# Three branch and output weight blocks loaded into the attention's room ahead of the row gathers, and heads 4 to 7 of both token halves projected from one load

## What is computed

```python
q, k, v, z, gl = split_proj(h @ w_in[l])
y = mix_branches(...)         # attention, gating; then @ w_branch_attn, w_branch_sgu, w_out
x_new = x + gt1 * rmsnorm(y, g_post_mix[l])
h2 = modulate(rmsnorm(x_new, g_pre_ffn[l]), sh2, sc2)
x = x_new + gt2 * rmsnorm(peer(h2, ...), g_post_ffn[l])

# peer: 8 heads, 256 queries wide each, 16 experts a head for every token
q = rmsnorm((xt @ w_query).reshape(T, 8, 2, 128))
s = einsum('thpd,pnd->thpn', q, sub_keys)
s1, i1 = top_k(s[:, :, 0], 16);  s2, i2 = top_k(s[:, :, 1], 16)
best, pos = top_k(all 256 sums s1 + s2, 16)
gate = softmax(best)
act = gelu(einsum('td,thkd->thk', x, u_tab[idx])) * gate
out = einsum('thk,thkd->td', act, v_tab[idx])
```

## Time and profile before

| | us |
|---|---|
| median of three runs | 2205.68 |
| lowest, highest | 2204.83, 2207.36 |
| the profiled execution, its whole time | 2205.23 |
| its span in the trace | 2203.4 |
| first row issued, last data of the rows | 1486, 2184 |

### The profile page before, as it was taken

How to read it: one execution, slowest core, us unless ns; L and a number is a source line. 1 busy time by engine, 2 the same in 40 slices (tenths; PEclk the granted TensorE clock), 3 DMA queues, 4 the chain that set the end, 5 groups by cost and what they waited for, 6 DMA issues and landing times.

```text
span 2203.4 us, 24558 instructions
## 1 busy us (share of the span) xinstructions
PE 1490.9 (68%) x10272; PEld 620.2 (28%) x10272; DVE 753.4 (34%) x1892; ACT 434.0 (20%) x992; POOL 291.8 (13%) x265
## 2 busy tenths in 40 slices
PE   8888766767775665666659999997756744344344
PEld 7554311322221111111114454555323511001000
DVE  5823101000000000000013143345657676876774
ACT  1321110000000000000011174342333232323221
POOL 0000000000000000000000000003434445444341
PEclk9988877888898878777879999998867865655555
DMA  9549999999999999999994346449999999999996
GB/s 387 210 174 397 427 426 426 426 428 427 427 427 427 427 427 426 427 427 427 427 418 162 152 185 235 178 166 410 422 421 402 419 420 420 417 420 419 419 419 279
DMA packets 75870, 814.24 MB, mean 370 GB/s; under 512 B 8464, under 2 KB 8592, under 8 KB 9840
## 3 DMA queue, kind: packets, MB, share of 16 engines
q1 hardware_dynamic: 38704, 544.03, 59.3%
q0 software_dynamic: 36864, 268.45, 29.4%
q10 hardware_dynamic: 192, 0.20, 0.0%
HBM read 811.40 MB, written 1.05 MB: 369 GB/s over the span
## 4 chain that ended last, share of the span: by engine, by line
DMA 48%; PE 33%; DVE 12%; ACT 4%; issue 2%; POOL 2%; ACTq 0%; DVEq 0%; POOLq 0%
DMA AR<-in_w_down 18%; DMA AR<-in_w_up 15%; DMA AR<-in_peer_uv,AR 14%; PE PS L396 13%; DVE AR L1384 3%; PE PS L624 3%; PE PS L829 3%; PE PS L645 2%; PE PS L787 2%; PE PS L407 2%; POOL AR L1761 2%; PE PS L511 1%; DVE AR L906 1%; DVE AR L908 1%; PE PS L657 1%
## 5 line engine op out<-in xcount | busy, mean ns | idle before, releaser
L1761 POOL DMA_INDIRECT AR<-in_peer_uv,AR x256 | 290.0, 1133 | 1704.9 <-DVE AR L1375 1438.3
L829 PE MATMUL PS<-AR 32*32 32x512 f32 x4096 | 233.2, 944 | 328.8 <-ACT AR L1720 328.8
L624 PE MATMUL PS<-AR 128*32 128x512 f32 x2048 | 301.9, 726 | 187.1 <-DMA AR<-in_w_up 131.9
L1384 DVE CUSTOM_DVE_ANT_0 AR<-AR 128x1024 f32<-128x1024 f32 x256 | 309.5, 1222 | 154.1 <-DMA AR<-in_peer_uv,AR 154.1
L396 PE MATMUL PS<-AR 128*128 128x512 f32 x736 | 330.8, 605 | 1.9 <-DVE AR L881 1.9
L645 PE MATMUL PS<-AR 128*32 128x512 f32 x1024 | 174.7, 818 | 102.4 <-DMA AR<-in_w_down 94.9
L1080 DVE TENSOR_TENSOR AR<-AR,PS 128x512 f32<-128x512 f32 x16 | 11.0, 688 | 596.6 <-PE PS L624 596.6
L396 PEld LDWEIGHTS PS<-AR 128*128 128x128 f32 x736 | 140.1, 195 | 173.2 <-issue 172.6
L624 PEld LDWEIGHTS PS<-AR 128*32 128x32 f32 x2048 | 63.2, 121 | 414.2 <-DMA AR<-in_w_up 207.5
L829 PEld LDWEIGHTS PS<-AR 32*32 32x32 f32 x4096 | 43.9, 128 | 474.1 <-ACT AR L1720 461.7
L1094 DVE COPY AR<-PS 128x512 f32<-128x512 f32 x16 | 11.1, 692 | 282.9 <-PE PS L645 282.9
(11 more groups left out here) (273 smaller groups left out, 1251.1 us busy)
## 6 DMA issues: line engine op xcount, KB each, us to landing
AR<-in_w_gate SPq DMA_DIRECT2D x64, 2048.0 KB, 26.1
AR<-in_w_up SPq DMA_DIRECT2D x64, 2048.0 KB, 25.7
AR<-in_w_down SPq DMA_DIRECT2D x64, 2048.0 KB, 26.4
AR<-in_w_in SPq DMA_DIRECT2D x29, 2048.0 KB, 7.8
AR<-in_w_ada SPq DMA_DIRECT2D x12, 2048.0 KB, 9.8
AR<-in_peer_w_query SPq DMA_DIRECT2D x8, 2048.0 KB, 11.9
AR<-in_w_out SPq DMA_DIRECT2D x6, 2048.0 KB, 11.5
AR<-in_w_branch_sgu SPq DMA_DIRECT2D x4, 2048.0 KB, 7.7
```

The costliest lines, as they stand in the source:

```text
L624: x = pe.matmul(PS[32 * q:32 * q + 32, bk, :], XS[:, j, e * 32:(e + 1) * 32], IN[key][:, jj, q * 512:(q + 1) * 512], start=(j == 0), stop= ...
L829: x = pe.matmul(PS[c:c + 32, ACC[a][g], :], DI[t, p, r, :], AR[t, off + 1024 + m * 512:off + 1536 + m * 512], start=(h == 0 and p == 0), s ...
L1384: v.tensor_tensor_reduce(rows, rows, HB[:, a, :], 1.0, 0.0, MULT, ADD, DOT[:, ix, k:k + 1]).then_inc(*w.hit("dot", ix, k))
L1761: pool.indirect_dma_start(out=AR[:, off:off + 2048], out_offset=None, in_=D["peer_uv_2"], in_offset=bass.IndirectOffsetOnAxis(ap=EI[:, ix, ...
```

## The change

What it does:

- Three loads, `w_branch_attn` 0 and 1 and `w_out` 0 for half 1, are issued as soon as the last attention head is done, ahead of the first row, into the places at W0, o and o + 16384. These hold the four row buffers of before.
- The row buffers in the beginning are instead one at o + 21120 and the eight halves of four weight slots: two slots that held query blocks 0 and 1, and two that held `w_branch_sgu` for half 1. That is nine again; a tenth comes after `yt` of half 1, and three more at `rt0` of item 8.
- Query blocks 2 and 3 (heads 4 to 7) are loaded once and used for both halves; the last load serving them is freed only by half 1. Blocks 0 and 1 are still loaded twice.
- `late` begins with the tail; the queries follow, first heads 4 to 7 with the halves alternating, then heads 0 to 3 of half 1, each `qs` joined with the next `qm`. 25 entries, popped after rows 0 to 72; the twelve queries stand after rows 30 to 63. `back` and `gain2` of half 1 are last.
- From the first row on there are five weight loads: `w_out` 1, query blocks 2 and 3, query blocks 0 and 1 again.

```diff
-        place = [NARENA + i * SLOT for i in range(NS)] + [W0, SPARE, o + 21120, o + 14336]
+        place = [NARENA + i * SLOT for i in range(NS)] + [W0, SPARE, o + 21120, o + 14336, o, o + 16384]
...
-            late = queries(2, 0) + queries(3, 0) + [h[0], h[1] + h[2]]
+            late = [h[0], h[1] + h[2]]
             late += [b[0][0], b[0][1] + b[1][0], b[1][1] + y[0], p[0][0], p[0][1] + p[1][0], p[1][1] + u[0], u[1] + u[2], u[3] + u[4]]
-            late += queries(0, 1) + [[("gain2",)], [("back", 1)]] + queries(1, 1) + queries(2, 1) + queries(3, 1)
+            late += queries(*[(h, a) for h in range(4, 8) for a in range(2)], *[(h, 1) for h in range(4)]) + [[("back", 1)], [("gain2",)]]
...
-            free = {k: ("mm", "av", 15) for k in (o + 2048, W0 + 2048, o + 16384, o + 18432)}
-            free[o + 21120] = ("gsb", 1, 1)
-            free.update({k: ("used", "wq", i, 0) for i in range(2) for k in halves[i]})
+            free = {o + 21120: ("gsb", 1, 1)}
+            for i, event in ((0, ("wq", 0, 0)), (2, ("w_bs", 0, 1)), (3, ("w_bs", 1, 1)), (1, ("wq", 1, 0))):
+                free.update({k: ("used", *event) for k in halves[i]})
...
-                key = ("wq", n, a)
+                key = ("wq", n, a if n < 2 else 0)
...
+                    for n in range(2):
+                        square(("wq", n, 0), "peer_w_query_2", n)
+                    w.wait_ge("mm", "av", 15)
+                    for slot, key, name, n in ((NS, "w_ba", "w_branch_attn_2", 0), (NS + 4, "w_ba", "w_branch_attn_2", 1),
+                                               (NS + 5, "w_op", "w_out_2", 0)):
+                        load(slot, (key, n, 1), weight(name, n), 8, 512)
+                    turn[0], ids[0] = 0, [NS, NS + 5]
-                elif stage == "ba":
+                elif stage == "ba" and x[1] == 0:
...
-                elif stage == "op":
+                elif stage == "op" and x != [0, 1]:
...
-                elif stage == "qm" and x[0] % 2 == 0:
+                elif stage == "qm" and (x in ([4, 0], [6, 0]) or x[0] in (0, 2) and x[1] == 1):
```

More of the change, by code:

```diff
@@ L289, in mixer_order, with queries @@
             steps(*u[2:4], pairs[9], u[4], pairs[10])
[L291 to L305, removed]
+            def queries(*heads):
+                parts = [[("qm", *heads[0])]]
+                for x, y in zip(heads, heads[1:]):
+                    parts.append([("qs", *x), ("qm", *y)])
+                return parts + [[("qs", *heads[-1])]]
             h, b, y, p, u = tail(1)
-            late = queries(2, 0) + queries(3, 0) + [h[0], h[1] + h[2]]
+            late = [h[0], h[1] + h[2]]
             late += [b[0][0], b[0][1] + b[1][0], b[1][1] + y[0], p[0][0], p[0][1] + p[1][0], p[1][1] + u[0], u[1] + u[2], u[3] + u[4]]
-            late += queries(0, 1) + [[("gain2",)], [("back", 1)]] + queries(1, 1) + queries(2, 1) + queries(3, 1)
+            late += queries(*[(h, a) for h in range(4, 8) for a in range(2)], *[(h, 1) for h in range(4)]) + [[("back", 1)], [("gain2",)]]
             todo += [("take", 0), ("qm", 0, 0), ("qs", 0, 0), ("rt0", 0)]
-            q = queries(0, 0)
-            for x in q[2:] + [[("back", 0)]]:
-                todo += x
+            todo += [("qm", 1, 0), ("qs", 1, 0), ("back", 0)]
             todo += [(f"rt{s}", 0) for s in range(1, 6)]
@@ L318, in mixer_order @@
             assert not then
-            for x in queries(1, 0):
-                todo += x
+            todo += [("qm", 2, 0), ("qs", 2, 0), ("qm", 3, 0), ("qs", 3, 0)]
             routes = []
@@ L343, in build @@
         ORDER = mixer_order()
+        HEADS = [tuple(x) for stage, *x in ORDER if stage == "qm"]
         RING = [5, 2, 3, 4]
@@ L352, in row_places @@
             halves = [[NARENA + i * SLOT, NARENA + i * SLOT + 2048] for i in RING]
-            free = {k: ("mm", "av", 15) for k in (o + 2048, W0 + 2048, o + 16384, o + 18432)}
-            free[o + 21120] = ("gsb", 1, 1)
-            free.update({k: ("used", "wq", i, 0) for i in range(2) for k in halves[i]})
+            free = {o + 21120: ("gsb", 1, 1)}
+            for i, event in ((0, ("wq", 0, 0)), (2, ("w_bs", 0, 1)), (3, ("w_bs", 1, 1)), (1, ("wq", 1, 0))):
+                free.update({k: ("used", *event) for k in halves[i]})
             bufs = list(free)
             for stage, *x in ORDER:
-                if (stage, *x) == ("rt0", 8):
-                    free.update({k: ("used", "wq", i, 1) for i in (2, 3) for k in halves[i]})
-                    bufs = bufs + halves[2] + halves[3]
+                new = {}
+                if (stage, *x) == ("yt", 1):
+                    new[o + 2048] = ("used", "w_ba", 1, 1)
+                elif (stage, *x) == ("rt0", 8):
+                    new = {o + 16384: ("used", "wq", 0, 1), o + 18432: ("used", "wq", 0, 1), W0 + 2048: ("used", "wq", 1, 1)}
+                free.update(new)
+                bufs += new
                 if stage == "row":
@@ L788, in qm @@
                                       HT[:, j, a * 128:(a + 1) * 128], start=(j == 0), stop=(j == 7))
-                x.then_inc(*w.hit("mm", "qp", h, a, also=[("used", *key)] if r else ()))
+                x.then_inc(*w.hit("mm", "qp", h, a, also=[("used", *key)] if r and (n < 2 or a) else ()))
             def qs(h, a):
@@ L795, in qs @@
                 for q in range(2):
-                    x = pe.matmul(PS[:, b, q:q + 1], SQP[:, h % 2, q * 128:(q + 1) * 128], ones[:, 0:1], start=True, stop=True)
+                    x = pe.matmul(PS[:, b, q:q + 1], SQP[:, HEADS.index((h, a)) % 2, q * 128:(q + 1) * 128], ones[:, 0:1], start=True, stop=True)
                 x.then_inc(*w.hit("mm", "rq", h, a))
@@ L1237, in row_of @@
                     w.wait_ge("mm", "av", 15)
+                    w.wait_ge("used", "wq", 1, 1)
                     for m in range(2):
@@ L1684, in qm @@
             def qm(h, a):
-                r = h % 2
+                i = HEADS.index((h, a))
                 d = QP[a][:, 2 * h:2 * h + 2, :]
@@ L1690, in qm @@
                 w.wait_ge("qp", h, a)
-                if (h, a) not in ((0, 0), (1, 0)):
-                    w.wait_ge("mm", "rq", *((h - 2, a) if h > 1 else (h + 6, 0)))
-                act.activation(SQP[:, r, :].rearrange("p (q t) -> p q t", q=2), d, ACT.Square).then_inc(*w.hit("qsq", h, a))
+                if i > 1:
+                    w.wait_ge("mm", "rq", *HEADS[i - 2])
+                act.activation(SQP[:, i % 2, :].rearrange("p (q t) -> p q t", q=2), d, ACT.Square).then_inc(*w.hit("qsq", h, a))
             def qs(h, a):
@@ L1851, in sync @@
                     assert turn[0] % 4 == 0
-                elif (stage, *x) == ("hn1", 1):
-                    turn[0], ids[0] = 0, RING[2:]
-                elif stage == "ba":
+                    for n in range(2):
[6 more added lines that the diff above has]
+                elif stage == "ba" and x[1] == 0:
                     square(("w_ba", *x), "w_branch_attn_2", x[0])
-                elif stage == "op":
+                elif stage == "op" and x != [0, 1]:
                     square(("w_op", *x), "w_out_2", x[0])
-                elif stage == "qm" and x[0] % 2 == 0:
+                elif stage == "qm" and (x in ([4, 0], [6, 0]) or x[0] in (0, 2) and x[1] == 1):
                     square(("wq", x[0] // 2, x[1]), "peer_w_query_2", x[0] // 2)
```

## The result

The changed kernel takes 2219.61 us (median of four runs, 2217.79 to 2223.45) against 2205.64 us before, a ratio of 1.0065 (95% interval 1.0047 to 1.0082). The time lies above the range of the prediction (2184 to 2209). The span of the profiled execution is 2221.6 us, 18.2 more than before.

What follows compares the result with a forecast made beforehand. The row phase was taken to be as long as its bytes, with `v` steps releasing rows until 1551 us. -25.1 + 14.5 + 4 - 2.4 = -9.0 us on 2205.23 gave 2196 us, range 2184 to 2209.

Steps and rivals of the forecast that it cites:

- The loads taken out: Row phase: ten weight loads become five, each worth 5.03 us at 417 GB/s; 25.1 us less.
- The early loads: Three loads ahead of the rows run from 1470.4 to 1485.5 us, inside a DMA hole; cost 0.
- The start: First rows, from 1488 us: DMA engines idle waiting for `v` steps and a projection; 14.5 us given back, bounds 7 and 20.
- What the queries cost: Twelve queries, one after every third row from row 30: 4 us lost, range 0 to 16.
- The slot: Three rows among the queries: 8.4 us of DMA against 7.8 us for PE, 9.2 with half at either clock.
- The low clock: Queries from row 30: at PE's low clock three rows need 10.6 us, with 5.01 us for a query.
- The cover: Among the queries: some four rows already in flight, 10 us, take nearly all of PE's 10 us excess.
- Rival 3: Queries between rows 30 and 66: PE falls below the DMA's pace, costing 16 us; 2212 us in all; chance 0.14.
- Behind row 72 nothing: Rows behind row 72: no dips of the DMA rate expected, 0 us.
- What goes with the old order: DMA hole between 1670 and 1680 us, where tail's end, a routing and a query met, disappears: -2.4 us.

Runs made afterwards that it cites:

- the two kernels above in which bytes or steps alone win nothing: Kernel before with two query-block loads beside the first rows cut to an eighth: 2204.78 us; kernel before with item 1's routing ahead of the rows: 2204.61 us.

## Why the prediction was wrong, step by step

- **The loads taken out, -25.1 us: right.** The balance of the spans closes to 0.2 us with it, and two loads put back cost 10.9 us (10.06 by the prediction's price) where the engines are full.
- **The early loads, 0: right.** Issued at 1467.9 to 1468.8 us, 421 GB/s from 1470 us.
- **The start, 14.5 us given back: right.** 15.9 measured. The third `v` step was put at 1529.2 and came at 1528.24:

```profile
1528.24 2.02 PE L823 MATMUL PS<-AR 32*32 32x512 f32 x32 [8.81 <-ACT AR L1715]
1530.20 8.55 PE L390 MATMUL PS<-AR 128*128 128x512 f32 x16
```

  The first branch projection took 8.55 us where I had 7.13. That the full share before 1551 hid a chain of steps is shown by the two kernels above in which bytes or steps alone win nothing.
- **What the queries cost, 4 us (0 to 16): here it failed.** 28.2 us were missing, 22.1 of them among the queries from 1610 to 1740 us (346 GB/s over 130 us). Three things in that step were wrong.
  - The slot. I summed PE's instructions and ACT's turn and had 9.2 us on average at mixed clock, 0.8 over the 8.4 of the DMA. Seven of eleven distances have 8.8, a little less than reckoned, but four have 12.7. They hold the table switches of the routing and the chain DVE - ACT - PE through them, which the sum left out, though the earlier trace rows showed two such loads in the start's chain. 4 x 3.9 = 15.6 us. The mean is then 10.2, and over the 8.4 it is 1.8 x 12 = 22 us. That it is the switches is read from the trace; no kernel here takes one out.
  - The low clock. The 5.01 us for a query at the low clock were run at a granted clock of 0.74. The slowest query of the changed kernel took 6.46 us, at 0.56 (1681.2 to 1687.5 us).
  - The cover. 10 us of rows in flight were set against the excess in full. The first deep dip (201 GB/s) comes already at 1620, some 10 us after the first query starts. The calm stretch from 1534 to 1551, on which I took 4 instead of the middle of the range, has no root in it, and weight loads beside it.
- **Rival 3** named the mechanism, its place and the point from which it decides (9.7 us in three rows), and had 0.14. The measured distance of 10.2 is beyond its point. Its price, 2212, was too low: 18 at the start measured 15.9, and 16 for the queries measured 28.2, or 22.1 without the dip of the next item.
- **Behind row 72 nothing: wrong.** `gain2` was passed over as a small step. It stands ahead of `rt4` of the next item, and POOL waited 12.17 us for that; the dip from 1750 to 1760 is 6.1 us of the 28.2. It isn't only that the kernel is late by then: with a query every fourth row, `gain2` again stands ahead of those indices (1752.47 us on DVE), POOL waits 13.68 us up to 1769.22, where the next item's wait is 8.00, and behind it comes

```profile
1770.00:1780.00 10.00, 7.96 (x132) 2.31 (x132) 8.35 (x18) 4.87 (x14) 6.96 (x6) 0.62 0.90 319
```

  That is 2.4 us. With a query every sixth row `gain2` falls later still; POOL waits 12.75 us up to 1850.70, and the ten us from there have 415 GB/s, no dip. So what `gain2` costs goes by where it stands. That the lateness of the changed kernel makes it larger is likely, but not shown by itself.
- **What goes with the old order, -2.4: of no weight.** The slice from 1670 to 1680 has 374 GB/s where it had 318, and deeper dips came beside it. The dips came from 1610 to 1740 and at 1750, where the prediction had 1585 to 1680.

## What to carry to other kernels

A full DMA share says only that the engines have work, not that their work sets the end: look at the chain of waits, and count bytes saved as time only in stretches where the chain runs over the DMA. When work is packed closer beside a stream, compare the distance of one packed unit with the DMA time of the rows beside it, and put into that distance the table switches and the waits for them that fall between, not only the instructions of the unit. Here one row more between two queries was worth 22 us, and 12 us of routing (with `hn1`) moved into waits ahead of the stream another 14.

## What the runs showed of the hardware

ACT's table loads took 1.28 us each, and the next instruction began 0.01 us behind (load at 1622.23, root at 1623.52 us), as in the earlier trace rows. The block projection of 16 records took 7.13 us at a granted clock of 1.00 (1539.8 us), and 8.55 us at 0.83 where PE had been waiting 8.81 us shortly before it (1530.20 us). A query took 3.82 us at 1.00 (1617.54 us) and 6.46 us at 0.56 (1681.12 us). So a stretch that PE enters from a wait cost more here than rows from a busy stretch say.

The DMA engines had a share of 1.01 in the first 70 us of the rows in the kernel before, and 8.8 us of bytes less there changed the time by nothing that can be told (ratio 1.0002); where the chain runs over the DMA, two loads more cost 10.9 us.
